# Two block-sum FFN stages of a two-block model: order of convolution taps, weight sums, splits and activation loads

## What is computed

```python
up = depthwise_conv(h @ w_up, conv_f_w, conv_f_b, 1)       # 3 taps over positions, 2 x 2816 channels
act = gelu(up[..., :2816], approximate=True) * up[..., 2816:]
x = x + act @ w_down
```

## Time and profile before

| | us |
|---|---|
| median of 3 runs | 3506.09 |
| lowest and highest | 3502.87, 3513.86 |
| the profiled execution | 3508.63 |
| its span in the trace | 3507.2 |

### The profile page before, as it was taken

One profiled execution on the slowest core, in us unless ns is written; L12 is line 12 of the kernel. 1 busy time (PEld: TensorE's weight loads), 2 busy tenths in 40 slices (PEclk: granted clock), 3 DMA queues, 4 the chain that ended last, 5 costly groups with the idle time before them and its releaser, 6 DMA issues.

```text
span 3507.2 us, 48868 instructions
## 1 busy us (share of the span) xinstructions
PE 3363.1 (96%) x19926; PEld 2726.0 (78%) x19926; DVE 2041.9 (58%) x2689; ACT 1388.7 (40%) x2361; POOL 1283.2 (37%) x698
## 2 busy tenths in 40 slices
PE   7999999999999899999999899999999999999999
PEld 6788888887668788878887677777788777777787
DVE  3665747337754733345555539985554677877554
ACT  4443433344433544421114547771232433343212
POOL 3212122110023444454441126662353455455442
PEclk9999999999999999999999999999999999999999
DMA  5111101110046344452222322223565333333422
GB/s 153 40 30 38 47 25 46 44 43 7 1 140 211 100 128 130 142 171 97 96 96 96 108 70 81 81 81 104 179 206 177 103 96 99 101 103 107 162 100 85
DMA packets 343792, 344.40 MB, mean 98 GB/s; under 512 B 14662, under 2 KB 263938, under 8 KB 343569
## 3 DMA queue, kind: packets, MB, share of 16 engines
q1 hardware_dynamic: 328960, 307.00, 27.6%
q10 hardware_dynamic: 11520, 25.17, 1.9%
q0 software_dynamic: 3088, 9.10, 0.7%
HBM read 268.86 MB, written 72.35 MB: 97 GB/s over the span
## 4 chain that ended last, share of the span: by engine, by line


## 5 line engine op out<-in xcount | busy, mean ns | idle before, releaser
L458 POOL TENSOR_TENSOR weight_lo<-stage,weight_hi 128x1024 fp32r<-128x1024 f32 (+4 forms) x269 | 615.4, 2294 | 1005.6 <-ACT weight_hi L436 976.9
L2447 DVE TENSOR_TENSOR x<-x,psum 128x512 f32<-128x512 f32 x416 | 284.1, 687 | 288.0 <-PE psum L403 266.5
L436 ACT ACTIVATE weight_hi<-stage 128x1024 fp32r<-128x1024 f32 (+4 forms) x329 | 298.4, 924 | 337.6 <-PE psum L403 289.4
L401 PE MATMUL psum<-hT_hi,weight_hi 128*128 128x512 f32 x1024 | 410.5, 401 | 1.5 <-DVE hT_lo L647 1.5
L402 PE MATMUL psum<-hT_lo,weight_hi 128*128 128x512 f32 x1024 | 399.8, 390 | 0.0
L403 PE MATMUL psum<-hT_hi,weight_lo 128*128 128x512 f32 x1024 | 399.6, 390 | 0.0
L401 PE MATMUL psum<-weight_hi,act_hi 128*128 128x512 f32 x864 | 339.6, 393 | 10.9 <-POOL act_lo L2395 7.9
L402 PE MATMUL psum<-weight_lo,act_hi 128*128 128x512 f32 x864 | 338.9, 392 | 0.0
L403 PE MATMUL psum<-weight_hi,act_lo 128*128 128x512 f32 x864 | 338.7, 392 | 0.0
L458 POOL TENSOR_TENSOR weight_lo<-sum,weight_hi 128x512 fp32r<-128x512 f32 (+1 forms) x114 | 217.4, 1913 | 275.9 <-ACT weight_hi L436 275.9
L401 PE MATMUL psum<-T_hi,weight_hi 128*128 128x512 f32 x608 | 239.8, 394 | 28.1 <-POOL weight_lo L458 24.1
(11 more groups left out here) (417 smaller groups left out, 7102.8 us busy)
## 6 DMA issues: line engine op xcount, KB each, us to landing
stage<-in_w_up SPq DMA_DIRECT2D x66, 512.0 KB, 4.0
stage<-in_w_in SPq DMA_DIRECT2D x64, 512.0 KB, 3.9
act_raw<-scratch_act SPq DMA_DIRECT2D x54, 512.0 KB, 5.4
stage<-in_w_ffn_up SPq DMA_DIRECT2D x48, 512.0 KB, 4.6
scratch_gates<-gate ACTq DMA_DIRECT2D x64, 256.0 KB, 2.0
gs<-scratch_gates SPq DMA_DIRECT2D x64, 256.0 KB, 2.9
stage<-in_w_out SPq DMA_DIRECT2D x32, 512.0 KB, 4.4
scratch_act<-out SPq DMA_DIRECT2D x64, 256.0 KB, 4.6
```

Of the source, the lines that this page charges most:

```text
L401: q.matmul(out, stat[0], mov[0], start=first, stop=False, skip_group_check=onto)
L436: a.q.activation(hi[:, part], src, ACT.Copy).then_inc(*S.w_hi.up(w))
L458: g.q.tensor_tensor(lo[:, part], src, hi[:, part].bitcast(F32), ALU.subtract).then_inc(*S.w_lo_pool.up(w))
L2447: v.q.tensor_tensor(dst, dst, K.bank(key), ALU.add).then_inc(*S.x.up(("f", f, g, t, n)))
```

## The change

In both stages: the third of the four sums, not the fourth, releases the high halves of parts 2 and 3; a new generator `up_norm` replaces the general one, with other places for `rstd`, `scale_rows` and `turn` of the second half of the rows; the step `released` behind the first splits moves ahead of the first product; the activation loads move from P6 of the last unit to P4 of the one before; the activation splits stand in front of the weight refill. In the second stage: `conv(u-1, 0)`, `raw_first(u)` and `gated(u-1)` move behind the refill at P7; `conv_first(u, 1)` moves behind the refill at P4; the last unit's convolution of its first block moves into the down rows, two and four row groups in.

```diff
--- before.py
+++ after.py
@@ -429,7 +429,8 @@
     if K.sums_of[w] is None:
         a.wait_ge(S.stage_load[K.load_of[w][0] % STAGES], K.load_of[w][0])
     else:
-        a.wait_ge(S.raw_sum, K.sums_of[w][0:2])
+        f, u, part = K.sums_of[w]
+        a.wait_ge(S.raw_sum, (f, u) if part == 4 else (f, u, 3))
     if K.slot_had[w] is not None:
         a.wait_ge(S.mm, ("tile", K.slot_had[w]))
     for part, src in split_sources(K, w):
@@ -3222,6 +3223,29 @@
         self.back += 1
         self.slot(self.slot_of[w])
 
+    def up_norm(self, nid):
+
+        self.do("scale_rows", nid, 0)
+        yield
+        for t in range(1, NT):
+            if t in (4, 6):
+                self.do("rstd", nid, range(t, t + 2))
+            self.do("scale_rows", nid, t)
+            if t > 4:
+                yield
+            if t < 5:
+                self.do("turn", nid, t - 1)
+                yield
+            elif t == 5:
+                for k in (4, 5):
+                    self.do("turn", nid, k)
+                    self.do("parts", nid, k)
+                    yield
+        for k in (6, 7):
+            self.do("turn", nid, k)
+            self.do("parts", nid, k)
+            yield
+
     def norm(self, nid, groups=((0, NT // 2), (NT // 2, NT)), first=0):
 
         for group in groups:
@@ -3233,11 +3257,7 @@
             for t in ts:
                 if t < ts[-1]:
                     self.do("scale_rows", nid, t + 1)
-                    if nid in UP_NORM and t >= NT // 2:
-                        yield
                 self.do("turn", nid, t)
-                if nid in UP_NORM and t >= NT // 2:
-                    self.do("parts", nid, t)
                 yield
 
 
@@ -3523,7 +3543,7 @@
 def order_merge(o, m, nid, branches, w_out, ahead=()):
 
     o.do("gain", nid)
-    norm = o.norm(nid, ((0, NT // 2), (NT // 2, NT // 2 + 2), (NT // 2 + 2, NT)), NT // 2)
+    norm = o.up_norm(nid)
     o.engines = ["G", "V"]
     slot = itertools.cycle(range(GATE_SLOTS))
 
@@ -3662,9 +3682,10 @@
     def low(name, *ts):
         for t in ts:
             o.do("split_lo", nid, name, t)
-    advance(norm, 2)
+    advance(norm, 1)
     for t in (LATE_ROWS[1], KEPT_ROW) + (RAW_ROWS if f == 2 else ()):
         o.do("spill", f, t)
+    o.released()
     product(0, "P1")
     advance(norm, 1)
     for name in ("T2", "T4", "B22", "T1", "T3"):
@@ -3672,7 +3693,6 @@
     for name in ("T4", "B22"):
         low(name, 4, 5)
     low("T2", 4, 5)
-    o.released()
     product(1, "P1")
     advance(norm, 1)
     low("T1", 4, 5)
@@ -3708,41 +3728,34 @@
                 if u == 0:
                     spent(EARLY - 1, "P2")
                     low("B22", 6, 7)
-                if f == 2 and u:
-                    o.do("conv", u - 1, 0)
-                if u == last:
-                    for i in range(4):
-                        o.do("act_load", f, i)
             elif name == "P5":
                 product(u, "P5", join=False)
             elif name == "P7":
                 product(u, "P7", join=False, back=False)
-                if f == 2 and u:
-                    o.do("raw_first", u)
                 o.do("join", f, u, "P7")
                 o.do("join", f, u, "P5")
-                if f == 2 and u:
-                    o.do("gated", u - 1)
-                spent(u, "P7")
                 if u == last:
                     for i in range(2):
                         o.do("act_split", f, i)
                     for t in SUM_ROWS[:2]:
                         o.do("x_back", f, t)
+                spent(u, "P7")
+                if f == 2 and u:
+                    o.do("conv", u - 1, 0)
+                    o.do("raw_first", u)
+                    o.do("gated", u - 1)
             elif name == "P4":
                 product(u, "P4", back=False)
+                if u == last - 1:
+                    for i in range(4):
+                        o.do("act_load", f, i)
+                spent(u, "P4")
                 if f == 2:
                     o.do("conv_first", u, 1)
-                spent(u, "P4")
-                if f == 2:
                     o.do("conv", u, 1)
             else:
                 product(u, "P3")
-    if f == 2:
-        o.do("conv_first", last, 0)
-        o.do("conv", last, 0)
-        o.do("gated", last)
-    for t in SUM_ROWS[2:] + LATE_ROWS + (KEPT_ROW,) + (RAW_ROWS if f == 2 else ()):
+    for t in SUM_ROWS[2:] + LATE_ROWS + (KEPT_ROW,):
         o.do("x_back", f, t)
     for i in range(2, 4):
         o.do("act_split", f, i)
@@ -3750,7 +3763,21 @@
     o.slot(RING - 1)
 
 
-def order_down(o, f, last_group, block_done):
+def conv_end(o):
+
+    last = UNITS_UP[2] - 1
+    yield
+    o.do("conv_first", last, 0)
+    o.do("conv", last, 0)
+    for t in RAW_ROWS:
+        o.do("x_back", 2, t)
+    yield
+    yield
+    o.do("gated", last)
+    yield
+
+
+def order_down(o, f, last_group, block_done, rest=iter(())):
 
     down, blocks = (o.io["w_ffn_down"][0], NF) if f == 1 else (o.io["w_down_2"][0], NF2)
     groups = blocks // GRP
@@ -3768,6 +3795,7 @@
                 if t == rows[-1]:
                     o.released()
                 o.do("down_rows", f, g, t, n)
+                advance(rest, 1)
         act_blocks(g)
     last_group()
     g = groups - 1
@@ -3974,7 +4002,7 @@
         if t in LAST_ROWS:
             order_rows(o, "out", LAST_ROWS[t])
     order_unit_up(o, 2, norm)
-    order_down(o, 2, lambda: o.do("gain", "out"), block_done)
+    order_down(o, 2, lambda: o.do("gain", "out"), block_done, conv_end(o))
     o.do("end")
 
 
```

## The result

The changed kernel takes 3591.51 us (median of four runs, 3588.73 to 3596.69) against 3506.34 (3502.87 to 3513.86) for the kernel before, run beside it: the ratio is 1.0245, with a 95% interval of 1.0225 to 1.0265. It is slower by 85 us. The profiled execution took 3593.58, its span is 3592.2, and the two profiled executions differ by 84.95.

A forecast was written before the change was run, and what follows sets the result against it. The prediction took PE, busy 96% of the span, as the bound. It summed 42 + 26 + 23 - 30 = +61 on 3508.63, giving 3570, or 3567 for a median, in a range of 3515 to 3600.

The forecast's parts named there:

- The hold of P1(u+4): Second stage, units 1 to 4: P1(u+4) waits for ACT's copy until 9.4 us after P7's end; +42 in sum.
- Units with the sums at P7: Second stage, units 7 to 10, 14 to 17, 20: serial chain delays P7's end to 21.2 or 22.3 us; together +26.
- Units with a P1 tile at P7: Second stage, units 5, 6, 11 to 13, 18, 19: moved work precedes the sums, P7 ends at 24.4; +23.
- The edges: Both stages' starts and ends: waits and the half clock behind them go; -30 in sum, bounds -15 to -40.
- (a): Both stages' entries: up_norm and earlier release remove waits for xn and the fourth unit's P1 tile; gain 9 and 11.
- (b): Stage 1's end: earlier activation loads and splits remove the 4.4 act_lo wait and 1.9 of half clock; gain 6.3.
- (c): Second stage's end: the 3.4 wait goes and row additions start earlier; of 4 us gained, 2 are left.
- (d): Stage 1: releasing at the third sum saves 0.6, removing three other low-half waits with their restarts; gain 1.5.
- The gain of the refill edits: Second stage: part 3's splits escape the right block's scaling (1.25 on ACT) but now stand behind raw_first and gelu.
- Rival 1: Second stage: DVE and POOL block less, taps run bare, the hold is 7.3; total 3500, chance 0.08.
- Rival 2: Second stage, units 1 to 4: taps are done in time, so ACT's copy does not hold P1; 3454, chance 0.08.
- Rival 3: Second stage: holds of 10.5, 5 us in each of 16 other units, edges only 15; 3627, chance 0.1.

The follow-up runs named there:

- port_bare: The changed kernel with POOL's weight low halves cut to 8 columns in units 1 to 21 of the second stage; 3507.81 us (one execution).
- acts_only: The changed kernel with the old order at P7 and the last unit's first activation splits in front of ACT's joins; 3472.48 us, ratio 0.9897 to the kernel before.
- weights_alone: The kernel before with only the third sum as releaser and the right block's scaling behind the refill at P4; 3496.21 us (one execution).
- undo_p7: The changed kernel with only the new order at P7 of the second stage put back to the old; 3474.73 us, ratio 0.9901 to the kernel before.
- move_alone: The kernel before with only the new order at P7 of the second stage; 3625.67 us, ratio 1.0335.

## Why the prediction was right, and where its sizes were off

The forecast was 3567, slower, in a range of 3515 to 3600; 3591.51 is inside and 24 above. Step by step:

- **The hold of P1(u+4)**: four holds of 9.3 to 9.5 us (predicted 9.4), half clock behind each: from P1's first matmul to the next product 5.1 to 5.3 us pass instead of 2.7, so 2.4 to 2.6 each (predicted 2.5). The stretch 1-4 grew by 42.4, predicted +42. The bare bound of 7.3 was found as 7.34 in port_bare. The rule of the Trainium skill (SBUF — State Buffer, Who interferes with whom) that was weighed there agrees with every row above, the second tap's 3.25 and the first sum's 2.81 among them.
- **Units with the sums at P7**: predicted 22.3 and 21.2. The six with a whole tile's low half between the taps have a mean of 23.0, the three others 21.9, some 0.7 more each. Behind P7(8), which ends at 3023.3, the chain went as worked out up to the scaling's end, at 13.5 against 13.4. Then the taps took 5.4 instead of 4.9, since POOL began a low half 0.3 ahead of the first as well (DVE, that place):

```profile
3036.82 2.07 DVE L2188 SCALAR_TENSOR_TENSOR xn<-raw,param,xn 128x1024 f32<-128x1024 f32 x1 [1.32 <-ACT xn L2180]
3038.93 3.30 DVE L2189 SCALAR_TENSOR_TENSOR xn<-raw,param,xn 128x1024 f32<-128x1024 f32 x1
```

- **Units with a P1 tile at P7**: predicted 24.4, measured 25.0 as a mean (24.9 from U3's join to the next). Two things make the difference. The chain runs some 0.2 late all along: in all seven units the low half of part 3 is ready 18.7 us behind the start of U3's join (18.9 behind P7's end was predicted), and in five of them P5 starts 0.14 later. The other is half clock, which I had counted behind waits over 3 us at the edges and behind the four holds, but not where my own chain made new waits of that size: P6 waits 3.6 for its low half in each of the seven. It costs less than it seems. P6(12) is at half clock and its twelve matmuls take 4.4 instead of 2.72; P6(19), behind the same wait, is at full clock, and P5(19) then waits instead (windows views of both, PE's row of P5(19)):

```profile
3107.30:3111.60 4.30, 4.30 (x12) 3.28 (x12) 3.71 (x3) 1.11 (x3) 4.30 (x3) 0.60 0.01 4
...
3272.90:3275.80 2.90, 2.81 (x12) 2.17 (x12) 2.86 (x2) 0.69 (x2) 2.90 (x2) 1.00 0.03 8
...
3277.42 0.47 PE L401 MATMUL psum<-T_hi,weight_hi 128*128 128x512 f32 x1 [1.43 <-POOL weight_lo L459]
```

  P5 starts 18.9 behind U3's join in both, and both units take 24.6 from join to join. Only behind P6(6) and P6(14), where half clock stretches the product to 5.3, P5 comes 0.8 later and the unit takes 25.5. With the item above, these 16 units cost 59 instead of 49.
- **The edges** were put at -30 and gave -19; this is the term with the largest error. In (a) and (b) it is one error made three times: a wait was counted as gone with its half clock, and what is late next was another step than the one I had named (a), or I had not asked for it (b). (a) Stage 1's entry: -5.7 for a predicted 9; the waits of 8.7 for xn and low halves are down to 1.3, but those for `kept` grew from 0.7 to 3.1. The second's: -7.3 for 11; P1(0) there waits 2.41 for the bank that ACT's squares (L2133) still use. (b) Stage 1's end: -2.2 for 6.3, since the split stands behind ACT's squares, which acts_only shows by gaining 3.4 more. (c) The second's end went the other way: -3.7 for 2. (d) The third sum in stage 1: 0 for 1.5, since P5 waits there for part 3 and not for part 2 (see weights_alone). None of this shortfall comes from the order at P7: undo_p7 has the same four edges within 0.6 us.
- **The gain of the refill edits** (third sum, scaling behind the splits) was said to be there but hidden by the chain. It is 14 us with the old order, and they take 18 off the loss with the new one, the differences of weights_alone to before and of after to move_alone.

Rival 1 (3500, the taps run bare) comes near port_bare, at 3507.81, and its condition does not hold in the real kernel. Its price for units 1 to 20 was +24 (28 + 10 - 4 - 10), against +21 in port_bare; that units 5 to 20 agree there (-10 and -12.4) is in part luck, since port_bare also takes away low-half time, which the rival did not. Rival 2 (3454, no hold) falls with the four waits of 9 us. Rival 3 (holds of 10.5, 5 us in every unit) falls too: no second low half got in between in units 1 to 4, and the other 16 lost 3.7 us each. What stays open: how port_bare's gain in units 5 to 20 divides between blocking and POOL's own time.

## What to carry to other kernels

Moving work off the front of a refill helps only if nothing on the in-order queues behind the refill frees a buffer that the next product writes: here PE's next product needed a bank that ACT frees, ACT's copy needed DVE's taps, and the taps had been put behind the sums and beside POOL. So list for each moved step who waits for its end, and look whether it used to run in a gap; DVE's gap before P7's end was free (PE never waited over 0.7 us for the copy), and the place behind the sums was dear. When several edits come together, take the one whose wait grows out and time the rest: here that turned +2.4% into -1%.

## What the chip showed that I had not expected

- Where a block between DVE and POOL is taken off one instruction, the next one gets it: product 3.35 and first sum 0.68 became first sum 2.81 and product 1.22, both 4.03 in sum.
- POOL's subtraction of 128x8 takes 0.20 us alone, that of 128x1024 2.40: 128 times the columns for 12 times the time. But however short, it waits for a DVE tap. port_bare's first, beside the tap of 2826.53, ends 0.06 behind it and takes 0.69; a later one is alone:

```profile
2827.18 0.69 POOL L461 TENSOR_TENSOR weight_lo<-sum,weight_hi 128x8 fp32r<-128x8 f32 x1 [11.70 <-ACT weight_hi L437]
...
2868.13 0.20 POOL L461 TENSOR_TENSOR weight_lo<-sum,weight_hi 128x8 fp32r<-128x8 f32 x1 [10.85 <-ACT weight_hi L437]
```

- What a wait costs in clock cannot be read from its length. Behind each hold of 9.1 us the twelve matmuls of P1 take 5.1 to 5.3 instead of 2.72. Behind waits of 3.6 us, six P6 take 4.3 to 5.3, and the seventh, P6(19), runs at full clock (above). Behind waits of 2.5 for `kept`, three P2 take 2.9, and the fourth, P2(18), takes 4.2 at a granted clock of 0.64:

```profile
3223.90:3228.10 4.20, 4.17 (x12) 3.42 (x13) 2.89 (x3) 3.20 (x4) 3.08 (x3) 0.64 0.31 125
```
